# Six waits and one set of copies moved in a two-block transformer kernel on one core

## What is computed

```python
h = x * (1.0 + sc1) + sh1
proj = h @ w_in[l]                                 # stage win
q_c, kv_c, k_r, r_q, r_k, r_v, r_g = jnp.split(proj, IN_OFFSETS, axis=-1)
q, k = rotary(r_q, pos), rotary(r_k, pos) * RET_DK ** -0.5   # stage rpre
scores = einsum('bhnid,bhnjd->bhnij', qc, kc) * decay        # stage ret; values vc
a = mla_mixer(q_c, kv_c, k_r, positions, ...)                # stage mla
y = jnp.concatenate([a, r], -1) @ w_out[l]                   # stage wf ...
x = layer_norm(ALPHA * x + gt1 * y, ln1_g[l], ln1_b[l])
h = x * (1.0 + sc2) + sh2
f = jnp.square(jax.nn.relu(h @ w_ff1[l])) @ w_ff2[l]
x = layer_norm(ALPHA * x + gt2 * f, ln2_g[l], ln2_b[l])
# first lines of the second block, for x and for the context xc:
u = rmsnorm(x, e_norm) * (1 + sc) + sh             # ... to here
# last line of all: return rmsnorm(x, final_norm)  # stage store
```

## Time and profile before

| | us |
|---|---|
| three runs | 2655.96, 2658.41, 2666.23 |
| median | 2658.41 |
| the profiled execution | 2656.23 |
| its span in the trace | 2654.4 |
| TensorE's mean granted clock | 0.971 of 2.4 GHz |

### The profile page before, as it was taken

One profiled execution on the slowest core, in us unless ns is written; L12 is line 12 of the kernel. 1 busy time (PEld: TensorE's weight loads), 2 busy tenths in 40 slices (PEclk: granted clock), 3 DMA queues, 4 the chain that ended last, 5 costly groups with the idle time before them and its releaser, 6 DMA issues.

```text
span 2654.4 us, 29005 instructions
## 1 busy us (share of the span) xinstructions
PE 2484.3 (94%) x11544; PEld 1938.4 (73%) x11544; DVE 1339.9 (50%) x1513; ACT 649.1 (24%) x944; POOL 734.7 (28%) x492
## 2 busy tenths in 40 slices
PE   5998889989899999999998699999998999999998
PEld 3786656657678888888786378885586778878876
DVE  7556744425624444344435779997528321324423
ACT  3002234422412101101123421113214200035510
POOL 1241320026453333333244111210045222340011
PEclk9999979999999999999999799999999999999999
DMA  6652000122132332332222121113232531110021
GB/s 228 200 164 65 20 19 9 56 71 80 56 119 76 95 95 76 88 100 90 78 92 74 35 95 46 40 32 111 76 112 83 166 75 47 47 40 1 1 88 71
DMA packets 228851, 206.96 MB, mean 78 GB/s; under 512 B 15248, under 2 KB 203280, under 8 KB 227712
## 3 DMA queue, kind: packets, MB, share of 16 engines
q1 hardware_dynamic: 223552, 178.61, 22.3%
q10 hardware_dynamic: 3840, 21.89, 2.1%
q0 software_dynamic: 1344, 4.91, 0.5%
HBM read 180.35 MB, written 17.83 MB: 75 GB/s over the span
## 4 chain that ended last, share of the span: by engine, by line
PE 78%; DVE 9%; issue 4%; ACT 4%; PEld 2%; DMA 1%; POOL 1%; PEldq 1%; SPq 0%; DVEq 0%; ACTq 0%; POOLq 0%
PE G L1654 28%; PE G L304 26%; PE G L1139 2%; PE M L307 2%; PE M L3041 2%; PE G L2546 1%; PE M L1689 1%; PE G L2362 1%; PE M L400 1%; PE M L2362 1%; DVE WMAX L3064 1%; PE M L1026 1%; PEldq L3187 1%; ACT WPT L3102 1%; PE G L2389 1%
## 5 line engine op out<-in xcount | busy, mean ns | idle before, releaser
L278 POOL TENSOR_SCALAR WH<-RAW 128x1024 fp32r<-128x1024 f32 (+1 forms) x156 | 136.4, 875 | 949.5 <-PE G L1654 517.6
L304 PE MATMUL G<-HH,WH 128*128 128x512 f32 x1056 | 336.6, 400 | 12.2 <-DVE HL L488 6.7
L304 PE MATMUL G<-HL,WH 128*128 128x512 f32 x1056 | 332.8, 396 | 0.0
L304 PE MATMUL G<-HH,WL 128*128 128x512 f32 x1056 | 331.9, 396 | 0.0
L281 POOL TENSOR_TENSOR WL<-RAW,WH 128x1024 fp32r<-128x1024 f32 (+1 forms) x156 | 304.6, 1953 | 13.0
L1654 PE MATMUL G<-HH,WH 128*128 128x512 f32 x624 | 221.3, 404 | 20.8 <-POOL WL L281 16.0
L304 PEld LDWEIGHTS G<-HH,WH 128*128 128x128 f32 x1056 | 188.3, 189 | 58.2 <-issue 13.4
L304 PEld LDWEIGHTS G<-HH,WL 128*128 128x128 f32 x1056 | 188.9, 188 | 42.2
L304 PEld LDWEIGHTS G<-HL,WH 128*128 128x128 f32 x1056 | 189.0, 189 | 41.5
L1654 PE MATMUL G<-HL,WH 128*128 128x512 f32 x624 | 217.7, 399 | 0.0
L1654 PE MATMUL G<-HH,WL 128*128 128x512 f32 x624 | 217.5, 398 | 0.0
(11 more groups left out here) (542 smaller groups left out, 4404.7 us busy)
## 6 DMA issues: line engine op xcount, KB each, us to landing
RAW<-in_w_ff SPq DMA_DIRECT2D x40, 512.0 KB, 4.0
RAW<-in_w_ff SPq DMA_DIRECT2D x80, 256.0 KB, 2.8
WVEC<-in_w_ada SPq DMA_DIRECT2D x24, 512.0 KB, 4.8
FVEC<-in_e_w_mod SPq DMA_DIRECT2D x24, 512.0 KB, 3.9
FVEC<-in_o_w_mod SPq DMA_DIRECT2D x24, 512.0 KB, 3.8
RAW<-in_o_w_in SPq DMA_DIRECT2D x24, 512.0 KB, 3.7
RAW<-in_e_w_in SPq DMA_DIRECT2D x20, 512.0 KB, 3.6
ADA<-in_w_ada SPq DMA_DIRECT2D x4, 2048.0 KB, 19.6
```

The lines of the kernel that those rows point to most:

```text
L278: pool.tensor_scalar(hi, raw, 1.0, 0.0, ALU.mult, ALU.add).then_inc(w_high, 1)
L304: m = pe.matmul(G[s][:, n * w:(n + 1) * w], part[s][:, k, :], acts[i][:, k, n * w:(n + 1) * w], start=first, stop=last)
```

## The change

Seven places:

1. `start`/`win`: DVE raises `ada_added` a second time when all eight HL tiles are done, and POOL's split of unit 1 waits for that.
2. `rpre`: the values are turned in G0 and G1; two of the four turns stand between the swaps. ACT copies them into VT once the fourth rotation has read the cosines. DVE no longer copies.
3. `ret`/`mla`: the rotary part of the query moves into `mla_first`, into M0, behind ACT's reading of the last turned head; the swapped part then goes to M1.
4. `wf`: SP's gate moves from i == 1 to i == 3, so that RAW of units 2 and 3 is loaded ahead of it; POOL's gate goes away.
5. `wf`, end: DVE takes "b" units out from f == 2 on rather than f == 4; ACT rounds the context inside `second_finish`, `context_low` follows the last "b" unit, and the first norm of the next block stands behind `center`. HHC and HLC change places.
6. `wf`, end: PE's sum for that norm moves from behind "b" unit 4 to behind unit 7, and ACT does both its tiles behind the root of half 1.
7. `oout`/`store`: the transposes of output tiles 0 and 1 move into a lead of `store`.

```diff
@@ start_dve @@
+            dve.wait_ge(S("li_lo"), KT)
+            dve.sem_inc(ada_added, 1)
@@ win_pool @@
-            pool.wait_ge(ada_added, 1)
             for j in range(16):
+                if j < 2:
+                    pool.wait_ge(ada_added, j + 1)
                 split_one(pool, r0 + j, u0 + j, KT)
@@ rpre_pe @@
+            def values_turn(j):
                 if j >= 2:
                     pe.wait_ge(S("rv_out"), j - 1)
                 for t in range(NT):
-                    m = pe.transpose(M[j % 2][:, t * P:(t + 1) * P], RV[:, j, t * P:(t + 1) * P], IDENT[:])
+                    m = pe.transpose(G[j % 2][:, t * P:(t + 1) * P], RV[:, j, t * P:(t + 1) * P], IDENT[:])
                 m.then_inc(S("rv_tr"), 1)
...
             pe.wait_ge(S("rr_rot"), 8)
+            pe.wait_ge(S("rr_mul"), 5)
             for j in range(2):
-                pe.wait_ge(S("rv_out"), 3 + j)
@@ rpre_act @@
             angle_table(act, ANGM[:], SINM, COSM)
+            act.wait_ge(S("rr_rot"), 7)
+            act.wait_ge(S("rr_sw"), 5)
+            for j in range(4):
+                act.wait_ge(S("rv_tr"), j + 1)
+                act.activation(VT[:, :, j * P:(j + 1) * P], G[j % 2][:].rearrange("p (t n) -> p t n", n=P), ACT.Copy)\
+                   .then_inc(S("rv_out"), 1)
@@ mla_first @@
             k_part(G[1], 0, mla_lead)
+            pe.wait_ge(S("ret_t32"), RET_HEADS)
+            q_part(M[0], WQR, 0, mla_lead)
@@ mla_pe @@
-            q_part(M[1], WQR, 0, S("ml_r"))
-            q_part(M[0], WQS, 0, S("ml_r"))
+            q_part(M[1], WQS, 0, S("ml_r"))
             v_part(0)
-            pe.wait_ge(S("ml_rot"), 2)
+            pe.wait_ge(S("ml_rot"), 1)
@@ wf_sp @@
-                if i == 1:
+                if i == 3:
                     gate(sp, current[0])
@@ wf_pool @@
-                if i == 2:
-                    gate(pool, current[0])
@@ wf_pe @@
-                     ("b", LAST, 4, 1): lambda: en_sum_pe(pe, 0)}
+                     ("b", LAST, 7, 1): lambda: en_sum_pe(pe, 0)}
@@ wf_act @@
                 second_finish(f, 0)
+                if f == 4:
+                    act.wait_ge(S("ff_lo"), len(A_AT))
+                if f in (4, 5):
+                    act.activation(HHC[:, 4 * f - 16:4 * f - 12, :], TCX[f - 4][:], ACT.Copy).then_inc(S("cx_hi"), 1)
             en_root(0)
+            squares("l2", 1)
+            root("l2", 1)
             en_tile(0, 0)
-            squares("l2", 1)
             en_tile(1, 0)
-            root("l2", 1)
-            for i in range(2):
-                act.activation(HHC[:, 4 * i:4 * i + 4, :], TCX[i][:], ACT.Copy).then_inc(S("cx_hi"), 1)
@@ wf_dve @@
-                if f >= 4:
-                    evict_ff(("b", LAST, f - 4, 1))
-                    gather_ff(f - 4, 1)
+                if f >= 2:
+                    evict_ff(("b", LAST, f - 2, 1))
+                    gather_ff(f - 2, 1)
@@ store @@
+        def st_first(pe):
+            for f in range(KT):
+                U_ = info("oout")["u0"] + f
+                pe.wait_ge(unit_freed[U_ % 2], U_ // 2 + 1)
+                for t in range(2):
+                    m = pe.transpose(M[t][:, f * P:(f + 1) * P], X[:, f, t * P:(t + 1) * P], IDENT[:])
+            m.then_inc(out_turned, 1)
```

More of the change, by code:

```diff
@@ L768, in rpre_pe @@
             pe.wait_ge(consts_in, 32)
-            for i, (tile, swap, _, _) in enumerate(turned):
-                swap_pe(pe, "rr", i, tile, swap[:])
-            for j in range(4):
-                pe.wait_ge(S("rr_mul"), 5 if j == 0 else 4)
+            def values_turn(j):
                 if j >= 2:
@@ L775, in rpre_pe @@
                 for t in range(NT):
-                    m = pe.transpose(M[j % 2][:, t * P:(t + 1) * P], RV[:, j, t * P:(t + 1) * P], IDENT[:])
+                    m = pe.transpose(G[j % 2][:, t * P:(t + 1) * P], RV[:, j, t * P:(t + 1) * P], IDENT[:])
                 m.then_inc(S("rv_tr"), 1)
+            for i, (tile, swap, _, _) in enumerate(turned):
+                swap_pe(pe, "rr", i, tile, swap[:])
+                if i in (1, 2):
+                    values_turn(i - 1)
+            values_turn(2)
+            values_turn(3)
             pe.wait_ge(S("rr_rot"), 8)
+            pe.wait_ge(S("rr_mul"), 5)
             for j in range(2):
-                pe.wait_ge(S("rv_out"), 3 + j)
                 for t in range(NT):
@@ L790, in rpre_dve @@
                 rope_dve(dve, "rr", i, tile, cos, sin, RTMP[:])
-            for j in range(4):
-                dve.wait_ge(S("rv_tr"), j + 1)
-                dve.wait_ge(S("rr_rot"), 10)
-                dve.tensor_copy(VT[:, :, j * P:(j + 1) * P], M[j % 2][:].rearrange("p (t n) -> p t n", n=P))\
-                   .then_inc(S("rv_out"), 1)
             dve.wait_ge(moved, info("rpre")["dma_end"])
@@ L1569, in build_program @@
         XC = Z("XC", [P, KT, CTX], F32, 28)
-        HHC, HLC = Z("HHC", [P, KT, CTX], F32R, 36), Z("HLC", [P, KT, CTX], F32R, 44)
+        HHC, HLC = Z("HHC", [P, KT, CTX], F32R, 44), Z("HLC", [P, KT, CTX], F32R, 36)
         CSPILL = nc.dram_tensor("c_spill", (P, KT, CTX), F32, kind="Internal").ap()
@@ L3128, in build_program @@
         OUT = [Z(f"OUT{s}", [P, D], F32, 16 + 4 * s) for s in range(N_OUT)]
+        out_turned = whole("out_turned")
+        def st_first(pe):
[5 more added lines that the diff above has]
+            m.then_inc(out_turned, 1)
         def st_pe(pe):
@@ L3133, in st_pe @@
             m.then_inc(S("st_ms"), 1)
-            for t in range(NT):
-                if t >= 2:
-                    pe.wait_ge(S("st_o"), t - 1)
+            for t in range(2, NT):
+                pe.wait_ge(S("st_o"), t - 1)
                 for f in range(KT):
@@ L3146, in st_dve @@
             for t in range(NT):
-                dve.wait_ge(S("st_tr"), t + 1)
+                dve.wait_ge(*((out_turned, 1) if t < 2 else (S("st_tr"), t - 1)))
                 if t >= N_OUT:
@@ L3161, in st_act @@
                 act.wait_ge(S(f"stored{s}"), 16 * (NT // N_OUT))
-        stage("store", dict(act=st_act, pe=st_pe, dve=st_dve))
+        stage("store", dict(lead=st_first, act=st_act, pe=st_pe, dve=st_dve))
         block = ctx.enter_context(nc.Block())
```

35 lines of the change are left out of this document (15 added, 20 removed).

## The result

The changed kernel takes 2638.51 us in the median of six runs (2633.44 to 2646.03), the kernel before 2657.73 in its six (2655.96 to 2666.23). The ratio is 0.9928, with a 95% interval of 0.9909 to 0.9948. So it is faster, by 19 us, and by more than half a per cent; but 37 us had been forecast, and the time lies 6.5 us above the range. The profiled execution took 2638.08 us, its span is 2636.3, against 2656.23 and 2654.4 before.

The account below looks back on a forecast made before the run. TensorE, busy 94%, was taken to wait at gates behind short serial chains. Gains of 1.4 + 4.2 + 5.7 + 11.4 + 12.9 + 1.3 = 36.9 us gave 2619.3, forecast as 2620 with half the run offset; range 2608 to 2632.

Parts of the forecast that it names:

- term 3: Start of mla: rotary query moved into the lead, both products ending at 337.8 instead of 343.47, 5.7 us saved.
- term 4: Start of wf: RAW loaded ahead of the gate, so unit 2 starts 9.3 us earlier and keeps its clock, 11.4 us saved.
- terms 5 and 6: End of wf: VectorE's chain 11.7 us shorter, plus 1.2 for the context no longer between two TN, 12.9 us saved.
- Terms 1 and 2: Unit 1's split behind the HL tiles in start/win, 1.4 us saved; values turned beside the rotation in rpre, 4.2 saved.
- What follows keeps its lengths: In mla, the instructions from the rotary products to the first scores were taken to shift earlier with unchanged durations.
- What is late next: Start of wf: VectorE's emptying of G0 was named as next late, by 0.2 us, leaving nothing more to get.
- rival B: Splits at wf's end hold VectorE in full, 10 us not 6, and win loses 1.4: 2625 to 2626; with smaller shortfalls 0.17.
- Term 7: Store: two output tiles turned ahead, sums 1.8 us faster at the high clock, 1.3 us taken, with 0 to 2.
- The base: The profiled execution of the kernel before, 2656.23 us, against which the sum of the gains was made.
- Rival C: One large wf place fails: unit 2 not held by RAW (2631), or VectorE's chain not by "b" units (2632); chance 0.13.

Follow-up runs that it names:

- quiet pair: b_spread and a_spread, the kernel before and the changed kernel, both with the modulation sums dealt out: 2648.98 to 2626.16 us.
- b_spread: The kernel before with only the 32 one-column products of five of the six modulation sums dealt out over eight units of wf each: 2648.98 us.
- a_spread: The changed kernel with the 32 one-column products of five of the six modulation sums dealt out over eight units of wf each: 2626.16 us.
- b_gates: The kernel before with only the changed gates at the start of wf (SP's gate moved, POOL's gone): 2651.95 us.
- bs_end: b_spread with only the two changes at the end of wf, including the exchange of HHC and HLC: 2642.98 us.
- best: The changed kernel with all six sums dealt out, GSL and BSL made earlier, unread products at wf's start and end, three output tiles turned in the store's lead: 2622.77 us.

## Why the prediction was wrong, step by step

The sum named 36.9 us. The quiet pair shows 22.8; the lines of the table give 5.6 + 3.5 + 7.0 + 6.3 - 1.2 = 21.2, and the store next to nothing. So the waits that the edits shorten were the right ones, and what failed are the sizes: term 3 was taken 2.2 us too large, term 4 4.4, and terms 5 and 6 together 7.8.

- **Terms 1 and 2, 5.6: right** (5.6 measured, on average over six and ten traces). They were not built apart, but the traces part them: rpre's first product starts at 246.6 on average where it was 247.7, 1.1 for term 1's 1.4; from there to the first QX it is 29.6 for 34.0, 4.5 for term 2's 4.2. In the two profiled executions alone it was 0.3 and 4.0.
- **Term 3, 5.7: mis-sized, 3.5.** I read 5.46 + 3.23 for the two products out of one execution; in b_spread they took 4.33 and 2.90. (The start to start of twelve at the high clock is 2.85 in the earlier trace rows, not 2.82.) The rest is a hold that I had not looked for, in a_spread (POOL, DVE):

```profile
333.28 2.35 POOL L1433 TENSOR_TENSOR KLT<-KR,KHT 32x1024 fp32r<-32x1024 f32 x1
```
```profile
333.15 1.22 DVE L1354 TENSOR_TENSOR QTMP<-M,SINM 128x1024 f32<-128x1024 f32 x1 [1.43 <-PE M L1037]
334.52 2.20 DVE L1357 TENSOR_TENSOR QROT<-QROT,QTMP 128x1024 f32<-128x1024 f32 x1
```

  The last instruction of the rotation moved forward, under a KLT of GpSimd that had ended when it came before, and takes 2.20 instead of 1.23: 1.0 us. "What follows keeps its lengths" was the step that failed.
- **Term 4, 11.4: mis-sized, 7.0.** That RAW was the cause was right. Three things were not: the lead's unit 0 was done 1.5 us later than I had put it, so the split began and ended 1.5 later; "VectorE empties G0 at 573.25" left out the 128x8 instruction under WL, 0.8 at the end; and the clock did fall in the gap of 3.99 us, which cost 1.8 in the changed kernel (40.97 for 39.2) and 2.7 in b_gates. The clock was my lower bound, 9.3, and even that was not low enough. "What is late next" was asked, but only of the work that I had in view.
- **Terms 5 and 6, 12.9: mis-sized, 6.3, of which 1.2 go again in the expansion.** The order and the place were right. Of the 11.7 us, 2.0 were in the profiled execution of before alone. The holds were 10.4 us in the stretch, not 6: the small WL cost 4.3, as the sum had them, but the two wide ones 5.2 where it had 1.6 (the TN of 2.88 and the two ER of 4.26 above), and GpSimd's roundings 1.0 more. That is rival B's figure, and I had given it less weight because evictions show no loss. They do not, but it is the other instructions that fill this list. And the sums of squares with their wait took 11.9 us rather than 10.2. The context's 1.2 is in the measured figure.
- **Term 7, 1.3: mis-sized, nothing that can be told from none.** From the last X to the end of the trace it is 23.29 us in before and 22.87 in after, but 22.82 in b_spread and 23.04 in a_spread. No run has edit 7 alone. The sums gained 1.6, where 1.8 had been worked out; the low-clock transposes took 1.05 of it back, which stood in the text as a possibility, and the last NR began 0.4 later.
- **The base.** 2656.23 was a good total made of bad pieces: low-clock losses in the stretches that I changed, which I booked as waits to be removed, and few of them in the 725 us where I changed nothing. The 3 to 4 us between the 22.8 and the 19 that were measured lie, as far as the traces show, in the rows of the sums. That part is chance or exposure, and stays open.

Rival B was the nearest, but it stopped at 2625: it took the right loss at one place only. Rival C's band, 2629 to 2640 with a chance of 0.13, holds the measured time, but by luck: neither of its two causes was there, since RAW did hold unit 2 up (7.0 us in b_gates) and the moved "b" units did shorten VectorE's chain (6.4 in bs_end). No case had "several terms short at once", and that is where the range failed.

## What to carry to other kernels

Before a difference of a few us is worked out from rows at two clock levels, look at more than one execution, and take a duration at the low clock as a price only where it is low every time. Where VectorE's two-input SBUF work is moved, lay GpSimd's instructions over the new place one by one, the smallest VectorE instruction included. A long row of one-column products inside a full run is cheap to deal out: in the changed kernel that won 12.8 us, more than any of the seven edits, and in the kernel before 9.6 by the medians or 7.4 by the ratio, about as much as edit 4 (7.0 or 8.0), the best of them. Deal out so that nothing comes to wait for the sum: in best it did.
